# Mixing stage of a two-block layer: predicated copies over half of the queries, and two levels copied as rectangles by ScalarE

## What is computed

```python
b = jnp.cumsum(lf_n, axis=2)
pair = b[:, :, :, None, :] - b[:, :, None, :, :]
decay = jnp.exp(jnp.where(causal[:, :, None], pair, -jnp.inf))
A = jnp.einsum('bhtd,bhsd,bhtsd->bhts', q_n, k_n, decay)
o = jnp.einsum('bhts,bhsv->bhtv', A, v_n) + jnp.einsum('bhtd,bhdv->bhtv', q_n * jnp.exp(b), S)
```

## Time and profile before

| | us |
|---|---|
| median of 3 runs | 2322.58 (2319.39 to 2328.41) |
| the profiled execution: its time | 2331.22 |
| its span, first to last instruction | 2329.4 |
| TensorE busy in the span | 2207.1 (95%) |
| VectorE busy | 1668.1 (72%) |
| ScalarE busy | 908.6 (39%) |
| GpSimd busy | 624.5 (27%) |
| the mixing stage, within the span | 286 to 500 |

### The profile page before, as it was taken

How to read it: one execution, slowest core, us unless ns; L and a number is a source line. 1 busy time by engine, 2 the same in 40 slices (tenths; PEclk the granted TensorE clock), 3 DMA queues, 4 the chain that set the end, 5 groups by cost and what they waited for, 6 DMA issues and landing times. The chain is left out here.

```text
span 2329.4 us, 31744 instructions
## 1 busy us (share of the span) xinstructions
PE 2207.1 (95%) x12633; PEld 1967.9 (84%) x12633; DVE 1668.1 (72%) x2778; ACT 908.6 (39%) x1191; POOL 624.5 (27%) x356
## 2 busy tenths in 40 slices
PE   5999889989999998999999899999999899889997
PEld 3888777867799998999999899999999777667775
DVE  6645677873589999889886788888887645656543
ACT  3322234433233333566663333333333434556432
POOL 0000042322347776323334333333331000000000
PEclk9999999999999999999999999999999999999999
DMA  7677400022247777899999999999998122111222
GB/s 263 214 236 240 160 35 1 2 73 73 91 131 237 246 240 234 322 356 338 354 354 388 349 361 352 362 351 354 358 354 300 57 83 89 55 38 56 80 91 73
DMA packets 177443, 486.13 MB, mean 209 GB/s; under 512 B 13648, under 2 KB 80336, under 8 KB 165776
## 3 DMA queue, kind: packets, MB, share of 16 engines
q1 hardware_dynamic: 140432, 349.87, 43.5%
q0 software_dynamic: 36864, 134.23, 15.4%
HBM read 429.52 MB, written 52.43 MB: 207 GB/s over the span
## 5 line engine op out<-in xcount | busy, mean ns | idle before, releaser
L1115 PE MATMUL ps<-h_high,u_high 128*128 128x384 f32 (+1 forms) x1216 | 426.7, 351 | 14.7 <-POOL u_low L1337 11.9
L1117 PE MATMUL ps<-h_high,u_low 128*128 128x384 f32 (+1 forms) x1216 | 419.7, 345 | 0.0
L1116 PE MATMUL ps<-h_low,u_high 128*128 128x384 f32 (+1 forms) x1216 | 419.7, 345 | 0.0
L1115 PE MATMUL ps<-w_high,v_high 128*128 128x384 f32 x1024 | 344.6, 336 | 7.7 <-DVE w_low L1771 7.7
L1116 PE MATMUL ps<-w_low,v_high 128*128 128x384 f32 x1024 | 343.8, 336 | 0.0
L1117 PE MATMUL ps<-w_high,v_low 128*128 128x384 f32 x1024 | 343.7, 336 | 0.0
L1502 ACT ACTIVATE v_high<-v_raw 128x2048 fp32r<-128x2048 f32 x64 | 122.6, 1916 | 348.9 <-PE ps L1117 341.5
L1115 PEld LDWEIGHTS ps<-h_high,u_high 128*128 128x128 f32 x1216 | 230.4, 189 | 27.4 <-POOL u_low L1337 13.9
L1115 PE MATMUL ps<-h_high,w_high 128*128 128x512 f32 x560 | 227.0, 405 | 18.0 <-DVE w_low L2354 4.7
L1117 PEld LDWEIGHTS ps<-h_high,u_low 128*128 128x128 f32 x1216 | 230.2, 189 | 7.7
L1116 PEld LDWEIGHTS ps<-h_low,u_high 128*128 128x128 f32 x1216 | 230.3, 189 | 7.1
(11 more groups left out here) (440 smaller groups left out, 4178.9 us busy)
## 6 DMA issues: line engine op xcount, KB each, us to landing
v_raw<-in_peer_v SPq DMA_DIRECT2D x64, 1024.0 KB, 6.3
w_raw<-in_w SPq DMA_DIRECT2D x94, 512.0 KB, 3.6
u_first<-in_uT SPq DMA_DIRECT2D x32, 1024.0 KB, 5.6
u_second<-in_uT SPq DMA_DIRECT2D x32, 1024.0 KB, 5.8
xT<-in_late_w SPq DMA_DIRECT2D x56, 512.0 KB, 4.4
gelu_up<-gelu SPq DMA_DIRECT2D x128, 192.0 KB, 6.2
gates<-gates_sb SPq DMA_DIRECT2D x12, 2048.0 KB, 9.8
weighted<-gelu_up SPq DMA_DIRECT2D x64, 384.0 KB, 6.6
```

Source lines behind the costliest of these rows:

```text
L1115: pe.matmul(out, wh, mh, start=start, stop=False)
L1116: pe.matmul(out, wh, ml, start=False, stop=False)
L1117: return pe.matmul(out, wl, mh, start=False, stop=stop)
```

## The change

The entries wanted at level s lie in the queries of one half of each pair of blocks only. The predicated copy now runs over these queries alone (`later`), 256 in place of 512 entries of each partition. At levels 6 and 7 (`BANDS`) the wanted entries of a tile are plain rectangles: two of 32 keys x 32 queries, or one of 64 x 64. `copied` is no longer called for these two levels. Instead ScalarE copies the rectangles, in the step of the level itself and not of the next one, one instruction for each rectangle with all four tiles of a head: 4 instructions at level 6 and 2 at level 7 for each unit.

```diff
+    BANDS = (6, 7)
...
+        def later(x, s, d):
+
+            return x.rearrange("p i (n two m) -> p i n two m", two=2, m=1 << (s - 1))[:, :, :, 1 - d, :]
...
+            def bands(unit, s):
+                d, rows = unit % 2, 1 << (s - 1)
+                act.wait_ge(level_cp, n_cp(unit, s - 1))
+                for h in range(HP):
+                    act.wait_ge(level_mm, n_mm(unit, s, h))
+                    for a in range(0, P, 2 * rows):
+                        key, asked = slice(a + d * rows, a + (1 + d) * rows), slice(a + (1 - d) * rows, a + (2 - d) * rows)
+                        last = act.activation(A[key, TILES * h:TILES * (h + 1), asked],
+                                              ps[key, 4 + h, :].rearrange("p (i t) -> p i t", t=P)[:, :, asked], ACT.Copy)
+                    last.then_inc(level_cp, 1)
...
+                    elif kind == "level" and s in BANDS:
+                        bands(x, s)
                     elif kind == "level" and s > LEV:
                         copies(x, s)
...
                     else:
                         dve.wait_ge(level_cp, n_cp(unit, s - 1, h))
-                        ins = dve.copy_predicated(
-                            dst, pred[:, d, s - 1, :].unsqueeze(1).to_broadcast([P, TILES, P]), src)
+                        m = 1 << (s - 1)
+                        own = later(pred[:, d, s - 1, :].unsqueeze(1), s, d)[:, 0].unsqueeze(1)
+                        ins = dve.copy_predicated(later(dst, s, d), own.to_broadcast([P, TILES, P // (2 * m), m]),
+                                                  later(src, s, d))
                     ins.then_inc(level_cp, 1)
...
-                if s - 1 <= LEV:
+                if s - 1 <= LEV and s - 1 not in BANDS:
                     copied(unit, s - 1)
```

## The result

The changed kernel is slower. In 6 executions its median was 2335.6 us against 2326.1 in 6 of the kernel before, a ratio of 1.0042 (95% interval 1.0029 to 1.0054). Measured twice more it gave 1.0037 (1.0023 to 1.0051) and 1.0027 (1.0016 to 1.0037). The forecast was 2321.6 us and no measurable change. A loss of 0.42% is under the 0.5% that the prediction took for measurable, but its interval lies clear of 1.00: the kernel before against itself gave 1.0003, known within 0.1%, so far less than 0.5% can be told.

The account below looks back on a forecast made before the run. TensorE was taken to set the pace. Terms of -3.2 (half copies), -0.3 (unit 0, levels 1 and 2), +2.8 (levels 6 and 7) and -0.25 (levels 7 and 8) gave -1.0 us: 2321.6 us, range 2313 to 2332.

Parts of the forecast that it names:

- The bound: Mixing stage: TensorE sets the pace, 4.49 us per single slot; removing all its waits on A_diag copies wins 9.4 us.
- The term of the slots of levels 6 and 7: Units 1 and 2: level 7 waits for ScalarE's rectangles, +1.4 us in each slot, +2.8 us together.
- The chain to the rectangles: Units 1 and 2: fx, item, exponential, scaling, then rectangles; level 7 starts at 382.03 instead of 380.61, +1.4 us.
- the step that lets the q product start at 377.08: Slot of levels 6 and 7: the first pair of copies, from 376.46, takes 0.62 us, so the q product follows then.
- the reason against it: Against a clock fall before level 7: one early case only, and a 0.80 us wait had left the clock at 1.00.
- The gain from the half copies: Four slots with two levels, neither copy of the first on ScalarE: the 0.80 us wait goes, 4 x -0.80 = -3.2 us.
- The rectangles' own length: ScalarE's rectangle copies at levels 6 and 7: 0.28 us for 128 elements, 0.38 us for 256.
- the cover in single slots: Unit 0's levels 6 and 7, unit 3's level 6: rectangles done at 3.5 us, TensorE's next level at 4.49; price 0.
- Levels 7 and 8 of unit 3: Stage's last slots: level 8 would start at 485.50 instead of 485.75, -0.25 us.
- The clock rival: Units 1 and 2, 2.2 us idle before level 7: the clock falls, 1.7 us lost each time, 2325.0 us; chance 0.17.
- the last two small terms: Unit 0's slot of levels 1 and 2, -0.3 us, and unit 3's levels 7 and 8, -0.25 us.
- The forecast gain of 1.0: Whole kernel: all terms together give -1.0 us, no measurable change, 2321.6 us against a median of 2322.6.

Follow-up runs that it names:

- rects_only: The changed kernel with the old predicated copies over all queries, levels 6 and 7 still as rectangles by ScalarE; ratio 1.0034 to the kernel before.
- filled_gap: The changed kernel with TensorE making the transposes four times over between the levels in the slots of levels 6 and 7; ratio 1.0025 to the kernel before.

## Why the prediction was wrong

*The bound* was right. TensorE has the pace: single slots still take 4.49 us, and with VectorE relieved of 18 us of copies nothing came off them.

*The term of the slots of levels 6 and 7* is where it failed: +2.8 us, measured +7.1. The mechanism was as described, and two sizes were off. The chain to the rectangles made level 7 of unit 1 start 2.0 us later instead of 1.4. Of the 0.6 missing, 0.3 lie in the step that lets the q product start at 377.08. GpSimd's row stood in the earlier trace rows, from 375.78 to 377.56; in the kernel before the product started behind it, at 377.71. Moved ahead, it meets it: above it starts at 375.45, GpSimd is done at 375.88, and the product ends at 376.43, 0.55 us after that. The Trainium skill (SBUF — State Buffer, Who interferes with whom) says that a VectorE instruction with two SBUF inputs contends with a GpSimd instruction that reads SBUF. The trace agrees: this product took 0.98 us in place of 0.67. The other 0.25 us are ScalarE's: 0.73 instead of 0.61 us before the rectangles, and 0.57 instead of 0.46 for two of them, since they didn't overlap.

The larger part, 1.5 to 1.7 us in each slot, is the clock. It was among the rivals, at the right price (1.7 us) and with a chance of 0.17. The step that failed is the reason against it, that a wait of 0.80 us had left the clock alone; that says nothing of a wait three times as long, and the only row of that size spoke for the fall. In all profiles here the idles of 2.66 to 3.07 us before level 7 (eight of eight) brought the clock down, and those of up to 1.68 us in the counted stretch didn't. In between the length doesn't decide: the idle of 2.17 us before level 8 of unit 3 left the clock at 1.00 in four profiles (the changed kernel's three and rects_only) and brought it down in the fifth (filled_gap). In the stage's first slots an idle of 1.72 us, the third within some 15 us, slowed level 1 of unit 0 in 11 of the 14 profiles (2.61 to 3.65 us instead of 2.02). So a price for 2.2 us of idle could only have been a chance, and no run here gives a length below which an idle is safe.

*The gain from the half copies* was forecast at 4 x 0.8 us and measured at 1.2. Levels of 4 and more queries a piece did what was said: 0.42 us a copy, and the slot of levels 5 and 6 won 0.59 of the 0.80; 0.23 us of wait was left, since its product for q, moved ahead, met GpSimd's kd as well (0.97 us instead of 0.68). Copies of levels 1 and 2, 16 of the 40, took 0.65 us each back to back, where full rows take 0.67, and both slots of levels 2 and 3 won 0.1. The slot of levels 3 and 4, where only the first pair of copies is of that kind, won 0.38. Here is one such slot and the next of the changed kernel (VectorE's timeline):

```profile
358.59 1.31 DVE L986 COPY_PREDICATED A_diag<-pred,ps 128x256 f32<-128x256 uint8 x2
361.77 1.30 DVE L986 COPY_PREDICATED A_diag<-pred,ps 128x256 f32<-128x256 uint8 x2
365.88 0.77 DVE L986 COPY_PREDICATED A_diag<-pred,ps 128x256 f32<-128x256 uint8 x2
```

I had argued from products over the same halves that gaps are free. They are, for those and for a plain copy, and for the source and the mask of this one.

*The rectangles' own length* was right (for 128 and 256 entries, groups by form of the changed kernel: count, busy us, mean ns):

```profile
L892 ACT ACTIVATE A_diag<-ps 32x128 f32<-32x128 f32 x16 | 4.3, 266 | 0.2
...
L892 ACT ACTIVATE A_diag<-ps 64x256 f32<-64x256 f32 x8 | 2.8, 374 | 5.1 <-PE ps L796 5.1
```

and so was the cover in single slots, which cost nothing. *Levels 7 and 8 of unit 3* gave +0.3 instead of -0.25 us, since the product for q met GpSimd's kd there too:

```profile
486.50 1.64 DVE L1017 TENSOR_TENSOR qd<-hq,fx 128x512 f32<-128x512 f32 x1
...
489.70 0.72 ACT L914 ACTIVATE s_sb<-s_sb,na_sums 128x512 f32<-128x512 f32 x1 [1.98 <-DVE na_sums L970]
...
490.97 1.13 PE L804 MATMUL ps<-qd,kd 128*128 128x128 f32 x8 [2.17 <-ACT A_diag L892]
```

The product for q, moved into GpSimd's kd, took 1.64 us instead of 0.67, and level 8 waits for what stands behind it.

So the sum -3.2 - 0.3 + 2.8 - 0.25 measured -1.2 + (no value, the first slots vary) + 7.1 + 0.3 = +6.2 us. The clock rival alone would have given +2.4; the rest is 0.9 for the chain, 2.0 for the half copies, and what the last two small terms missed.

The 14.0 us between the forecast of 2321.6 and the 2335.6 measured hold more than the change. The forecast stood on a median of three runs of the kernel before, 2322.6; six give 2326.1, which is 3.5 us by the draw of runs alone. The forecast gain of 1.0 and the 6.2 measured in the stage make 7.2, and the other 3.3 us are placed by no trace here.

## What to carry to other kernels

When work is handed to an engine with time to spare, count what stands ahead of it in that engine's queue and what those instructions wait for; here 1.5 us of ScalarE's work, itself waiting for VectorE, stood ahead of 0.6 us of copies, and putting the copies first turned +6.2 us into -5, 2 of them in the last slots. A new gap in TensorE's stream can have two prices, the wait and the clock behind it. An earlier row with a gap of that size is better evidence than one with a shorter gap, but one row isn't enough: a gap of 2.17 us had both outcomes here. When a VectorE instruction moves to an earlier time, look at which GpSimd instruction it now meets.

## What was unexpected of the hardware

A predicated copy from PSUM to SBUF paid for small pieces of its destination alone: 0.73 us for 256 fp32 entries in pieces of 1 or 2, 0.44 us in pieces of 4 or dense, whatever the gaps in source and mask. The same idle of TensorE, 2.17 us, was followed by a fall of the clock in one profile of five. A product of VectorE with two SBUF inputs that starts under a GpSimd product took 0.98 to 1.64 us instead of 0.67, and ended 0.55 us after GpSimd did. A predicated copy from SBUF beside GpSimd's bias addition took 2.94 us and ended 0.6 us after it; whether it is slow by itself no run shows.
